# A causal hybrid decoder layer on one Trainium2 core: first queries and keys of three branches moved into the gate stage's block products

## The chip, the cores and the metric

One core of one Trainium2 chip runs the whole layer as one program. The metric is the device time of an execution in microseconds. Engines: PE (TensorE), DVE (VectorE), ACT (ScalarE), POOL (GpSimd) and SP (SyncE, which issues most DMAs).

## The reference

Input x is 1024 tokens by 1024 channels, fp32. One layer is x <- LN(a x + mixer(x)), then x <- LN(a x + ConvGLU(x)). The mixer runs four attention branches of 8 heads of 64 on one projection x W_in:

- A: window of 128 keys, 2 key heads, learned sinks, distance penalty;
- B: mixture of three dilations, own keys per head;
- C: each query takes its 256 best keys by an indexer score; one key and value head for all 8 query heads (`k` and `v` stand side by side in W_in, so one tile of 128 columns holds both);
- D: forgetting attention, with a cumulative log gate as bias.

Each branch's 512 outputs go through a projection to 1024 channels and are multiplied by sigmoid(x W_gate + b_gate) of that branch; the four products are summed and go through W_out.

```
proj   = einsum('bsnk,nkd->bsnd', branches, w_branch)
gates  = sigmoid(x @ w_gate + b_gate).reshape(b, L, 4, 1024)
merged = sum(gates * proj, axis=2);  y = merged @ w_out
```

## The kernel before, in words

fp32 precision is reached with pairs: every operand of a matmul is split into a high part (ACT copies it to fp32r, `*_hi`) and a low part (DVE or POOL subtracts, `*_lo`), and each product is three matmuls (high*high, high*low, low*high) of 128x128 by 512 columns. A projection of 128 output channels for all 1024 tokens (`project_parts`, L911) is 8 blocks of the inner size x 3 x 2 halves = 48 matmuls.

The order of the work is a written list, `STEPS` (`steps()`): x, indexer, `scores` (the indexer's scores), `gates`, then for each branch in the order B, D, A, C: first queries and keys (`q`, `k`; for C `kv_c` and `q`), values (`v` or `v_c`), four `attn` steps (one for a pair of heads), `osplit`, `merge`. Then `outproj`, `up`, `down`. Every engine's program walks the same list; engines meet only at semaphores, and each engine takes its own instructions in order.

**Gate stage** (`gates`, PE at L1225). The gate logits are made two tiles of 128 channels at a time (`GATE_TILES`, 22 tiles, 11 pairs) by block products: seven products of 12 matmuls each, with sums of weight blocks (POOL, `gate_weight_sums`) and of token blocks (made once), where two plain projections would take eight times 12. DVE combines the products (five operations a pair, L2694), ACT applies the sigmoid, SP stores the tile to DRAM. Between its combinations DVE runs parts of C's top-k search (`topk_parts`, `TOPK_GATES`: 14 parts a pair): the search has 191 parts, and 36 more (`topk_distances`, six per block of queries, six blocks of 384 to 1024 columns) turn the scores into distances. What the gate stage doesn't hold of them is spread over the merges (`TOPK_MERGE`) and the first projections (`TOPK_FIRST`).

**A branch's beginning.** PE projects the first queries and keys into two-bank PSUM tiles `pair[0]` and `pair[1]`; ACT scales and writes the high part into `heads` (`q_hi`, `k_hi`, L1675), DVE the low part (`q_lo` L2519, `k_lo` by `lo_part` L2648; each key row block twice, r = 0, 1). They read PSUM. Then `v`: of the value projection's eight parts of 6 matmuls PE runs five, the scores of unit 0, two more parts, the scores of unit 1, and the rest. A unit is 128 queries of one head; DVE adds its bias and takes the row minimum (`biased`, L2504), ACT exponentiates (`exps`, L1777), DVE takes the reciprocal (`inverse`, L2514), POOL normalises (L2230), PE transposes (L1000), ACT and DVE split the transposes (`pt_hi`, L2578), PE multiplies with the values (L1021). Projections of the next pair of heads are the filler between these (L927, plans `BESIDE`). For C there is no `v` projection: the key/value tile is staged and transposed (`v_c`, L963), four filler parts of 3 matmuls follow (`FIRST_C`), then the first units.

**Merge.** PE multiplies the branch's output with `w_branch` (L1247, L1254, L1271): eight tiles of 24 matmuls in four PSUM places; DVE multiplies each tile with its gate (L2957) and, for D and A, adds it to the sum `mid` (L2962). Gate tiles come back from DRAM into `prob[:, 0:2]` and `o_t[:, 0:4]` (`gate_home`, loads at L1476). Weights of the ring come through `w_raw` (SP, L1410), are split by ACT (L1652) and POOL (L2175), each tile as soon as the one two places earlier is used up: ACT splits one more as soon as the merge's last tile is done.

PSUM tile `pair[0]` holds the scores of one or two units: a unit marked by `scores_beside` waits until all but the last unit before it were read by `biased`, any other until all were.

## Time and profile before

| | |
|---|---|
| time, median of 3 runs | 2093.43 us (2091.26 to 2094.61) |
| profiled execution, its own time | 2093.97 us |
| its span | 2092.2 us |
| busy: PE, DVE, ACT, POOL | 2060.4, 1536.4, 968.5, 937.3 us |
| granted PE clock, mean | 0.999 |

How to read it: PE, DVE, ACT and POOL busy times are sums over instructions; a share of the span says little about a stage. The chain that ended last says which engine each moment of the span hangs on. Matmuls overlap: a row's mean duration is longer than the step from one matmul to the next, so PE's pace is read from a stretch and its count. A wait is put down to the engine whose signal came last.

### The profile page before, as it was taken

Reading aid. Unit: us, or ns where it says so; the run is one execution under the profiler, and the core shown is the slowest. Engines: PE = TensorE matmul, PEld = TensorE weight load, DVE = VectorE, ACT = ScalarE, POOL = GpSimd, SP = SyncE. Lnnn points to the kernel's source line nnn. Section 1 sums busy time; section 2 is a strip of 40 time slices with the busy share of each in tenths; the row PEclk is TensorE's granted clock in tenths of the full one; section 3 lists DMA queues with packets and bytes.
Section 4 is the critical chain, followed back from the end, with each engine's and each line's share of the span. In section 5 each row is a group of like instructions: output and inputs, shape, how many; then the busy total and the mean of one; then the engine's idle time right before and its main releaser. Section 6 shows DMA issues by size and latency. Waiting matters only on the chain.

```text
span 2092.2 us, 28999 instructions
## 1 busy us (share of the span) xinstructions
PE 2060.4 (98%) x10382; PEld 1727.0 (83%) x10382; DVE 1536.4 (73%) x2549; ACT 968.5 (46%) x1740; POOL 937.3 (45%) x796
## 2 busy tenths in 40 slices
PE   9999999999999999999999999999999999999998
PEld 7788888888888888888888888888788888888887
DVE  8678887777686666797785666668877777775668
ACT  5543334566615556615635666523433333344540
POOL 4287752333322223324523333524756565645651
PEclk9999999999999999999999999999999999999999
DMA  4233323110042111230031000441566665558862
GB/s 132 72 111 110 101 91 62 31 31 21 26 152 64 50 32 51 75 100 28 22 121 31 21 21 11 141 161 61 180 181 203 191 192 161 171 189 310 270 215 92
DMA packets 197373, 224.26 MB, mean 107 GB/s; under 512 B 25704, under 2 KB 149608, under 8 KB 197232
## 3 DMA queue, kind: packets, MB, share of 16 engines
q1 hardware_dynamic: 194320, 212.43, 32.7%
q10 hardware_dynamic: 2912, 10.00, 1.3%
q8 instruction: 83, 1.36, 0.3%
q14 instruction: 58, 0.48, 0.1%
HBM read 164.17 MB, written 58.23 MB: 106 GB/s over the span
## 4 chain that ended last, share of the span: by engine, by line
PE 87%; DVE 7%; issue 2%; ACT 2%; POOL 1%; DMA 0%; DVEq 0%; ACTq 0%; POOLq 0%
PE pair L1359 13%; PE pair L927 13%; PE pair L911 7%; PE pair L1225 7%; PE obank L1359 5%; PE pair L1388 5%; PE obank L1021 4%; PE chunk L1000 4%; PE pair L1318 3%; PE chunk L1388 3%; PE obank L1225 3%; PE pair L972 3%; PE pair L973 3%; PE pair L1271 2%; PE obank L1388 2%
## 5 line engine op out<-in xcount | busy, mean ns | idle before, releaser
L2175 POOL TENSOR_TENSOR w_lo<-w_raw,w_hi 128x1024 fp32r<-128x1024 f32 x64 | 159.5, 2492 | 311.1 <-ACT w_hi L1652 311.0
L1675 ACT ACTIVATE pt_hi<-chunk 128x512 fp32r<-128x512 f32 (+1 forms) x272 | 150.8, 555 | 179.2 <-PE chunk L1000 177.8
L2578 DVE TENSOR_TENSOR pt_lo<-chunk,pt_hi 128x512 fp32r<-128x512 f32 (+1 forms) x272 | 173.2, 638 | 80.1 <-ACT pt_hi L1675 75.7
L2230 POOL TENSOR_SCALAR prob<-prob,att 128x256 f32<-128x256 f32 (+4 forms) x172 | 118.1, 696 | 198.5 <-DVE att L2514 198.2
L927 PE MATMUL pair<-act_hi,w_hi 128*128 128x512 f32 x432 | 186.4, 432 | 2.5 <-DVE heads L2519 2.3
L927 PE MATMUL pair<-act_hi,w_lo 128*128 128x512 f32 x432 | 170.0, 393 | 0.0
L927 PE MATMUL pair<-act_lo,w_hi 128*128 128x512 f32 x432 | 169.4, 392 | 0.0
L2399 DVE TENSOR_SCALAR_CACHE_REDUCE o_top<-score,stat 128x384 uint8<-128x384 f32 (+1 forms) x186 | 167.0, 941 | 0.5
L1021 PE MATMUL obank<-pt_hi,heads 128*128 128x256 f32 (+1 forms) x568 | 148.4, 285 | 0.6 <-DVE pt_lo L2578 0.6
L1777 ACT ACTIVATE prob<-prob,att 128x257 f32<-128x257 f32 (+6 forms) x172 | 120.5, 702 | 39.3 <-DVE att L2504 38.0
L1021 PE MATMUL obank<-pt_lo,heads 128*128 128x256 f32 (+1 forms) x568 | 138.6, 281 | 0.0
L972 PE MATMUL pair<-heads 128*128 128x512 f32 (+3 forms) x352 | 119.9, 347 | 5.7 <-DVE att L2504 4.8
L911 PE MATMUL pair<-act_hi,w_hi 128*128 128x512 f32 x288 | 116.8, 405 | 5.0 <-DVE act_lo L2648 2.7
L1652 ACT ACTIVATE w_hi<-w_raw 128x1024 fp32r<-128x1024 f32 x64 | 67.4, 1053 | 111.8 <-PE obank L1271 38.3
L1000 PE MATMUL chunk<-ident,prob 128*128 128x128 f32 x660 | 111.9, 274 | 2.7 <-DVE pt_lo L2578 2.1
L1021 PEld LDWEIGHTS obank<-pt_lo,heads 128*128 128x128 f32 x568 | 108.2, 190 | 6.8
L1021 PEld LDWEIGHTS obank<-pt_hi,heads 128*128 128x128 f32 x568 | 107.4, 189 | 7.7 <-DVE pt_lo L2578 1.1
L973 PE MATMUL pair<-heads 128*128 128x512 f32 (+3 forms) x352 | 113.1, 334 | 0.0
L911 PE MATMUL pair<-act_lo,w_hi 128*128 128x512 f32 x288 | 112.6, 391 | 0.0
L911 PE MATMUL pair<-act_hi,w_lo 128*128 128x512 f32 x288 | 111.0, 392 | 0.0
L2230 POOL TENSOR_SCALAR mid<-mid,att 128x384 f32<-128x384 f32 (+4 forms) x56 | 37.8, 683 | 162.4 <-DVE att L2514 162.4
L927 PEld LDWEIGHTS pair<-act_hi,w_lo 128*128 128x128 f32 x432 | 81.1, 188 | 18.6
(489 smaller groups left out, 5932.5 us busy)
## 6 DMA issues: line engine op xcount, KB each, us to landing
down_sums<-dn_sums SPq DMA_DIRECT2D x40, 512.0 KB, 6.4
w_raw<-in_w_in SPq DMA_DIRECT2D x37, 512.0 KB, 3.8
gates<-o_t SPq DMA_DIRECT2D x22, 512.0 KB, 2.9
up_raw<-in_w_up SPq DMA_DIRECT2D x22, 512.0 KB, 4.8
gate_raw<-in_w_ffn_gate SPq DMA_DIRECT2D x22, 512.0 KB, 6.0
hidden<-gelu_s SPq DMA_DIRECT2D x22, 512.0 KB, 3.3
dn_raw<-down_sums SPq DMA_DIRECT2D x44, 256.0 KB, 4.1
h_in<-down_sums SPq DMA_DIRECT2D x44, 256.0 KB, 4.8
```

The source lines that it names most:

```text
L911: last = nc.tensor.matmul(dst[0:cols, s:s + HALF], w[:, k, :], a[:, k, s:s + HALF], start=(i == 0), stop=(i == len(order) - 1))
L927: last = nc.tensor.matmul(pair[1][:, s:s + HALF], w[:, k, :], a[:, k, s:s + HALF], start=(k == 0 and n == 0), stop=(k == NKT - 1 and n == 2))
L972: nc.tensor.matmul(dst[:, s:s + m], q, k_hi[:, s:s + m], start=True, stop=False)
L973: last = nc.tensor.matmul(dst[:, s:s + m], q, k_lo[:, s:s + m], start=False, stop=not masked)
L1000: last = nc.tensor.transpose(t[:, at:at + P], prob_slot(br, 2 * j + w)[:, s:s + P], ident[:])
L1021: last = nc.tensor.matmul(obank[bank_of(br)[j] % 2][:, q0:q0 + width], v, part[:, slot, at:at + width], start=(c == 0 and b == 0 and w == ...
L1225: last = nc.tensor.matmul(place, w[:, tokens_of(k)], gate_tokens(p, part, k), start=(p in (1, 6, 5) and k == 0 and m == 0), stop=(k == 3 a ...
L1359: last = nc.tensor.matmul(dst, w[:, cols], moving, start=(p in (1, 6, 5) and k == 0 and m == 0), stop=(k == 3 and m == 2), skip_group_chec ...
L1388: last = nc.tensor.matmul(banks[t], l[:, t * P:(t + 1) * P], r, start=(p in (6, 1, 5, 3) and k == 0 and m == 0), stop=(k == KFF - 1 and m ...
L2175: nc.gpsimd.tensor_tensor(split_into(1, g), w_raw[:, g % 2, 0:kt * cols], split_into(0, g).bitcast(F32), ALU.subtract).then_inc(lo_ready, 1)
L2399: nc.vector.tensor_scalar(junk[:, b % 2, 0:(i + 1) * P], s, limit if isinstance(limit, float) else limit[:, b:b + 1], None, ALU.is_ge, ALU ...
L2578: nc.vector.tensor_tensor(pt_lo[:, n % PT_SLOTS, 0:m], t[:, 0:m], pt_hi[:, n % PT_SLOTS, 0:m].bitcast(F32), ALU.subtract).then_inc(chunk_f ...
```

## The change

- `GATE_TILES` gets six more tiles, `HEAD_TILES`: queries and keys (for C the key/value tile) of D, A and C, the first 128 columns of each. They are made in the gate stage by block products, in three more pairs (14 in all), copied without the sigmoid, and stored to a DRAM tensor `first_heads`.
- The steps `q`, `k`, `kv_c` of D, A and C are replaced by a step `heads`. SP loads the two tiles into `o_t[:, 0]` and `o_t[:, 1]` once the fourth tile of the running merge is gated. ACT waits for the end of the merge on PE and writes the high parts: columns 0 to 511 of the first head and its keys, then 512 to 1023, then the second head and its keys. DVE writes the low parts in the same order, with the merge's last gated tile after the first half; then in `v`: other half, unit 0, second head, unit 1, reciprocal, staging copy. For C: first half, last gated tile, `v_c`, units 0 and 1, other half, second head, reciprocal, units 2 and 3. A semaphore `first_placed` counts these three pieces; PE waits for them before units 0, 4 and 8.
- PE starts the value projection right after the merge, and the scores of unit 0 stand after three of its parts for D and A instead of five.
- The whole top-k search is in the gate stage. Of the distance parts 24 (four blocks) stand in B's merge, 12 in D's, none in A's. POOL's sinks and bias for A wait for single gated tiles of D. ACT's spill of the last tile of B's merge moves behind the first heads' halves.

```diff
-TOPK_MERGE = {B: (2, 3), D: (1, 2), A: (0, 1), C: (0, 0)}
-TOPK_FIRST = {("k", D): 7, ("q", D): 6, ("k", A): 5, ("q", A): 5}
+EARLY_ROWS = 4
+LATE_DISTANCES = 5
+ROWS_BESIDE = 6
...
+HEAD_TILES = [(what, br) for br in BRANCH_ORDER[1:] for what in ("q", "k")]
+GATE_TILES = [(br, dt) for br in BRANCH_ORDER for dt in STORED_GATES[br] if (br, dt) not in FILLER_GATES] + HEAD_TILES
...
+        out += [("q", br, 0), ("k", br, 0)] if br == B else [("heads", br)]
...
                 if (br, pr) == (C, 0):
                     fill(FIRST_C)
+                    pe.wait_ge(first_placed, placed_first(br, 1))
                     scores(br, pr, 0)
                     scores(br, pr, 1)
...
+                        if p == 0 and br != B and u in (4, 8):
+                            pe.wait_ge(first_placed, placed_first(br, u // 4 + 1))
...
-                if merge_tiles.n and kind in ("q", "k", "kv_c", "outproj"):
+                if merge_tiles.n and kind in ("v", "v_c", "outproj"):
                     pe.wait_ge(merge_free, merge_tiles.n - 1)
...
                 elif kind == "v":
                     tile = project_parts(1, act_hi, act_lo)
-                    for _part in range(NKT // 2 + 1):
+                    for _part in range(NKT // 2 + 1 if step[1] == B else NKT // 2 - 1):
                         next(tile)
+                    if step[1] != B:
+                        pe.wait_ge(first_placed, placed_first(step[1], 1))
                     scores(step[1], step[2], 0)
...
+            def load_heads(br):
+                at = BRANCH_ORDER.index(br) - 1
+                if at == 0:
+                    sp.wait_ge(merge_free, 4)
+                else:
+                    sp.wait_ge(sum_done, sums_of(BRANCH_ORDER[at]) + 4)
+                for what in ("q", "k"):
+                    tile = GATE_TILES.index((what, br))
+                    sp.wait_ge(gate_stored[tile % 2], 16 * (tile // 2 + 1))
+                    sp.dma_start(first_head(what), tile_kept((what, br))).then_inc(heads_loaded, 16)
...
+            def first_heads(br):
+                at = BRANCH_ORDER.index(br)
+                act.wait_ge(merge_full, NKT * at)
+                act.wait_ge(heads_loaded, 32 * at)
+                first_half(br, 0)
+            def first_half(br, s):
+                q_hi(br, 0, 0, first_head("q")[0:HD, half_cols(s)], half_cols(s))
+                k_hi(0, first_head("k")[0:HD, half_cols(s)], cols=half_cols(s))
+            def other_heads(br):
+                first_half(br, 1)
+                if br == D:
+                    act.wait_ge(merge_free, merge_at(B) + NKT)
+                    spill(NKT - 1)
+                q_hi(br, 0, 1, first_head("q")[HD:P, :])
+                if br != C:
+                    k_hi(1, first_head("k")[HD:P, :])
...
-                    if step[:2] == ("k", A):
+                    if step == ("heads", A):
+                        pool.wait_ge(sum_done, sums_of(D) + NKT - 2)
+                        make_bias(0)
+                        pool.wait_ge(sum_done, sums_of(D) + NKT - 1)
+                        set_sinks(0, 0)
                         pool.wait_ge(sum_done, sums_of(D) + NKT)
...
+            def first_half(br, s):
+                q_lo(br, 0, 0, first_head("q")[0:HD, half_cols(s)], half_cols(s))
+                k_lo(0, first_head("k")[0:HD, half_cols(s)], cols=half_cols(s)).then_inc(first_placed, 1)
+            def first_heads(br):
+                before = BRANCH_ORDER[BRANCH_ORDER.index(br) - 1]
+                first_half(br, 0)
+                gated(before, NKT - 1)
+                dve.wait_ge(merge_free, merge_at(before) + NKT)
+                if before != B:
+                    dve.wait_ge(sum_done, sums_of(before) + NKT)
+            def other_head(br):
+                last = q_lo(br, 0, 1, first_head("q")[HD:P, :])
+                if br != C:
+                    last = k_lo(1, first_head("k")[HD:P, :])
+                last.then_inc(first_placed, 1)
...
                 elif kind == "v":
+                    if step[1] != B:
+                        first_half(step[1], 1)
+                    biased(step[1], step[2], 0)
+                    if step[1] != B:
+                        other_head(step[1])
+                    biased(step[1], step[2], 1)
+                    inverse(step[1], 0)
...
+                        if br == B and dt < ROWS_BESIDE:
+                            topk_parts(EARLY_ROWS * DISTANCE_PARTS // ROWS_BESIDE)
+                        elif br == D:
+                            topk_parts(((NSC - EARLY_ROWS) * DISTANCE_PARTS - LATE_DISTANCES) // (NKT - 1))
```

## Rows read from the trace of the kernel before

**Rows 1.** The page's first and fourth parts: busy time; the chain that ended last, by engine.

```profile
PE 2060.4 (98%) x10382; PEld 1727.0 (83%) x10382; DVE 1536.4 (73%) x2549; ACT 968.5 (46%) x1740; POOL 937.3 (45%) x796
...
PE 87%; DVE 7%; issue 2%; ACT 2%; POOL 1%; DMA 0%; DVEq 0%; ACTq 0%; POOLq 0%
```

**Rows 2.** What PE waited for (us in total, times, longest us); the largest.

```profile
PE pair L972 <- DVE att L2504: 4.8, 12, 0.8
```

**Rows 3.** Stretches: us, busy us of each engine (instructions), granted clock, DMA share, GB/s.

```profile
105.00:314.44 209.44, 209.44 (x925) 173.42 (x925) 178.74 (x426) 77.82 (x121) 151.09 (x118) 1.00 0.34 104
...
571.78:615.58 43.80, 43.80 (x195) 36.17 (x195) 36.22 (x71) 9.32 (x10) 9.65 (x4) 1.00 0.55 181
615.58:637.35 21.77, 21.77 (x97) 18.03 (x97) 18.82 (x42) 4.06 (x4) 4.81 (x2) 1.00 0.37 120
637.35:650.93 13.58, 13.16 (x64) 10.26 (x63) 7.07 (x11) 7.53 (x10) 3.21 (x3) 1.00 0.15 39
876.87:920.84 43.97, 43.90 (x193) 35.93 (x193) 40.88 (x46) 9.15 (x10) 10.48 (x4) 1.00 0.57 192
...
1098.26:1120.03 21.77, 21.77 (x99) 17.98 (x98) 8.41 (x6) 4.17 (x4) 4.80 (x2) 1.00 0.18 49
```

**Rows 4.** The page's sixth part: DMA issues, KB each, us from issue to landing.

```profile
w_raw<-in_w_in SPq DMA_DIRECT2D x37, 512.0 KB, 3.8
```

**Rows 5.** DVE's timeline in D's merge, distance parts: start us, us, instruction.

```profile
928.17 1.01 DVE L2441 TENSOR_SCALAR_CACHE_REDUCE o_top<-score,stat 128x768 uint8<-128x768 f32 x1
...
931.86 1.02 DVE L2452 SCALAR_TENSOR_TENSOR prob<-aux,stat,prob 128x768 f32<-128x768 f32 x1
```

**Rows 6.** ACT's timeline at B's merge end and in D.

```profile
615.67 1.06 ACT L1652 ACTIVATE w_hi<-w_raw 128x1024 fp32r<-128x1024 f32 x1 [9.82 <-PE obank L1271]
...
667.49 1.19 ACT L1675 ACTIVATE heads<-pair 64x512 fp32r<-64x512 f32 x2
```

**Rows 7.** DVE's timeline in D, A and C.

```profile
668.78 1.38 DVE L2648 SCALAR_TENSOR_TENSOR heads<-pair,heads 64x512 fp32r<-64x512 f32 x2 [0.80 <-ACT heads L1675]
...
933.97 4.93 DVE L2648 SCALAR_TENSOR_TENSOR heads<-pair,heads 64x1024 fp32r<-64x1024 f32 x4 [1.08 <-ACT heads L1675]
...
952.63 0.48 DVE L2504 CUSTOM_DVE_ANT_0 prob<-pair,o_t,sink_neg 128x256 f32<-128x256 f32 x1 [0.77 <-PE pair L973]
...
954.01 1.23 DVE L2889 COPY prob<-pair 128x1024 f32<-128x1024 f32 x1
...
1098.40 1.22 DVE L2957 TENSOR_TENSOR prob<-obank,prob 128x1024 f32<-128x1024 f32 x1 [2.65 <-PE obank L1271]
1099.66 3.32 DVE L2962 SCALAR_TENSOR_TENSOR mid<-mid,prob 128x1024 f32<-128x1024 f32 x1
...
1126.18 0.54 DVE L2504 CUSTOM_DVE_ANT_0 aux<-pair,score 128x384 f32<-128x384 f32 x1
...
1126.64 0.68 DVE L2504 CUSTOM_DVE_ANT_0 prob<-pair,score 128x512 f32<-128x512 f32 x1
```

**Rows 8.** POOL's timeline at the ends of B's and A's merge.

```profile
616.81 2.41 POOL L2175 TENSOR_TENSOR w_lo<-w_raw,w_hi 128x1024 fp32r<-128x1024 f32 x1 [8.48 <-ACT w_hi L1652]
...
1099.50 2.40 POOL L2175 TENSOR_TENSOR w_lo<-w_raw,w_hi 128x1024 fp32r<-128x1024 f32 x1 [8.48 <-ACT w_hi L1652]
```

**Rows 9.** DVE's sums, L2962: ns least/median/most, first and last start.

```profile
L2962 DVE SCALAR_TENSOR_TENSOR mid<-mid,prob x8: 1224/1226/3382, 887.4 to 1099.7; 128x1024 f32<-128x1024 f32 x8
```

**Rows 10.** PE's timeline: A's first transposes and filler, C's first and fifth score.

```profile
954.95 0.55 PE L1000 MATMUL chunk<-ident,prob 128*128 128x128 f32 x3 [0.51 <-POOL prob L2230]
955.29 0.49 PE L927 MATMUL pair<-act_hi,w_hi 128*128 128x512 f32 x1
...
1123.73 0.33 PE L972 MATMUL pair<-heads 128*128 128x128 f32 x1
...
1127.39 0.50 PE L972 MATMUL pair<-heads 128*128 128x512 f32 x1 [0.76 <-DVE att L2504]
```

**Rows 11.** The last stretch of the span, columns as in rows 3.

```profile
2080.00:2092.20 12.20, 4.72 (x21) 3.57 (x19) 8.44 (x16) 0.41 (x2) 0.00 (x0) 0.91 0.27 105
```

More of the change, by code:

```diff
@@ L794, in gate_bias_of, with tile_weights, tile_kept, first_head @@
             return gate_bias[:, br * NKT + dt:br * NKT + dt + 1]
+        def tile_weights(tile):
+            if tile not in HEAD_TILES:
+                return w_tile(w_gate[0], tile[0] * D_MODEL + tile[1] * P, P)
+            what, br = tile
+            return w_tile(w_in[0], Q_COL[br] if what == "q" else CK if br == C else K_COL[br], P)
+        def tile_kept(tile):
+            return heads_dram[HEAD_TILES.index(tile)] if tile in HEAD_TILES else gates_dram[tile]
+        def first_head(what):
+            return o_t[:, 0 if what == "q" else 1, :]
+        def placed_first(br, part):
+            return 3 * (BRANCH_ORDER.index(br) - 1) + part
         gate_out = [o_t[:, 2, :], o_t[:, 3, :]]
@@ L1518, in _ @@
                                  allow_slow_non_contiguous=True).then_inc(late_params, 16)
+                if step[0] == "heads":
+                    load_heads(step[1])
                 for n, source in enumerate(ring_sources(step)):
@@ L1726, in gate_operands, with gate_made_of @@
                     nc.scalar.activation(gate_operand(q, 0), gate_source(n, p), ACT.Copy).then_inc(gate_op_hi, 1)
+            def gate_made_of(n, k, dst, src):
+                tile = GATE_TILES[2 * n + k]
+                if tile in HEAD_TILES:
+                    return nc.scalar.activation(dst, src, ACT.Copy)
+                return nc.scalar.activation(dst, src, ACT.Sigmoid, bias=gate_bias_of(*tile))
             def take_first(n):
@@ L2832, in _ @@
                         counted(9)
-                    topk_parts(TOPK_FIRST.get(step[:2], 0))
-                    if step == ("q", D, 0):
-                        dve.wait_ge(pair_free[0], tiles[0].n)
-                        signal().then_inc(bias_used, 2)
                     k = step[1] in (B, D)
@@ L2969, in merged_lo @@
                     def merged_lo(k):
                         lo_part(act_lo[:, k, :], mid[:, k, :], act_hi[:, k, :]).then_inc(split_done, 1)
-                    topk_parts(start_parts)
-                    for dt in range(NKT):
+                    if br == D:
+                        topk_parts(LATE_DISTANCES)
+                    elif br == A:
+                        own(nc.vector.tensor_copy(dist_a[:], dist[:, SEQ - 2 * P:SEQ]))
+                    for dt in range(NKT if br == FINAL else NKT - 1):
```

188 lines of the change are left out of this document (79 added, 109 removed).

## The prediction

> **What bounds the kernel now.** I read the page first: PE is busy 98% of the span and carries 87% of the chain that ended last, DVE 7% [rows 1]. So PE work taken away is time, if nothing new makes PE wait. PE's waits are small: its largest, for DVE's biased scores, is 4.8 us in all [rows 2]. Then the table by stretch: the gate stage runs 924 matmuls of 128x512 in 209.44 us, and the 96 of D's first queries and keys take 21.77 us with PE never idle [rows 3]; both give 0.2268 us a matmul. (The rows' mean of some 0.39 us is latency, not the price.) In the same table DVE is busy 36.22 of 43.80 us in B's merge, but only 8.41 of the 21.77 us after A's merge: there queries and keys of C shelter a nearly idle DVE. Last I read the timelines around the three merge ends, since the change removes just this shelter. Below, T is the end of a merge on PE: 615.58 us (before D), 920.84 (A), 1098.26 (C) [rows 3].
>
> **Projections.** Removed: six projections (queries and keys of D and A, queries and the key/value tile of C) of 48 matmuls = 288 x 0.2268 = 65.3 us. Added: six tiles = three pairs of seven products of 12 matmuls = 252, 57.2 us. Sum: minus 8.16 us. Each new pair brings DVE five combinations and 14 search parts, ACT and POOL seven operands, POOL four sums; that is the load of the eleven pairs of now, which all run at PE's pace (19.04 us a pair, 209.44 / 11), so I charge nothing. If that cover failed, the excess of one engine over 19.04 us would be paid three times; no row shows an excess. The same three pairs swallow the 39 search parts that now stand in the merges, and the last pair has three parts fewer, which only moves work under B's first projection, again full.
>
> **Queues.** SP stores six more tiles of 512 KB in the gate stage and loads them again, each pair of loads behind the fourth gated tile and ahead of the value weights. With 5.44 us of PE a merge tile (24 matmuls) that is some 18 us before T. A load of 512 KB lands in 3.8 us [rows 4], and ACT splits the value weights two tiles, 11 us, before T, so all three are there; cost 0. Cover gone, ACT's placing would be late by what is missing, and then the first score unit. D's bias loads queue behind them, with 10 us to spare. ACT's fourth spill moves behind half of its placing; the D step waits there for the last gated tile. POOL's sinks and bias for A now follow its weight split; needed only some 8 us later: 0.
>
> **Merges.** B's merge gives DVE 24 distance parts in place of 26 search parts; four parts of the widest row, 768 columns, run from 928.17 to 932.88, 4.7 us [rows 5]. With the gating of 1.2 us that is 5.9 us against 5.44 us of PE a tile, but narrower rows go first, and my tally for six tiles (22 us of parts, 8 us of gating, 2 to 4 us of blocks as below) ends with the seventh tile gated about 1 us before T. The value projection waits for that tile. I take 0, with 2 us as the other end. D's merge has 12 parts instead of 17, A's none instead of 8: 0.
>
> **The merge ends.** Here is the cost. Once PE is done (T), ACT first splits a weight tile (615.67, 1.06 us) and only then can place; one half of the first queries and keys is three operations of 0.6 us, so ACT ends at T+2.8 [rows 6]. DVE's low parts of the same half are three of 0.61 to 0.69 us (two took 1.38 us) [rows 7]. They now read both operands from SBUF, where the removed ones read PSUM. And POOL subtracts the same weight tile from T+1.23 to T+3.64 [rows 8]. A DVE sum of two SBUF tensors takes 1.23 us alone, and 3.32 us when it starts beside such a subtraction, ending 1.1 us after it [rows 7 to 9]. So DVE's first low part ends at T+4.2 and the half at T+5.5; without the block it would be T+4.15. The nearest rows have 128 partitions, not 64; I take the block, since every sum that met a subtraction shows it, and keep 1.3 us as the other end.
>
> What the row shows, the Trainium skill's page "SBUF — State Buffer", section "SBUF: two separate sides", states as a rule: a VectorE operation with two SBUF inputs and a GpSimd operation that reads SBUF take one port pair for the whole instruction, and the loser fully blocks. By it the sum is the one with the block, whatever the partitions; without it each transition would be 1.3 us cheaper.
>
> **D.** PE needs the first half at T+4.08 (18 matmuls) and gets it at T+5.5: 1.4 us lost. The value projection then ends at T+13.0. DVE meanwhile: gating to 6.7, other half to 8.7, unit 0 to 9.1, then the other head, three operations of 1.2 us, waiting for ACT (10.3 after its own spill) to 12.8, unit 1 to 13.2. ACT's exponential, reciprocal and POOL's normalising follow as in A, where the transposes begin 1.8 us after unit 1's sum (953.1 to 954.95) [rows 7, 10]: here at T+15.1, where scores 2 and 3 end at 14.0. Another 1.1 us. Now PE loses 0.4 us in this stretch (busy 13.16 of 13.58 us) [rows 3]. Net 1.4 + 1.1 - 0.4, rounded up for semaphores: +2.2 us.
>
> **A.** The same, and DVE's sum of the last tile of D (1.2 us) also stands ahead. First unit: 1.4 us lost, value projection ends at T+12.8. DVE: gating and sum to 8.0, half to 10.0, unit 0 to 10.4, other head to 14.0, unit 1 to 14.6, reciprocal 15.5, staging copy (1.23 us) to 16.7 [rows 7]. PE stands before score 3 until 14.6, before the transposes until 16.3 and before the filler until 16.7, that is 3.9 us after the projection's end, where it now is 1.4 us (two scores 0.5, wait 0.51, transposes 0.34) [rows 10]. Net 1.4 + 2.5 = +3.9 us.
>
> **C.** No value projection shelters anything: transposes and 12 filler matmuls end at T+3.8, in the trace 3.7 us from 1120.03 to 1123.73 [rows 3, 10]. The first half comes at T+5.5 (+1.8). Then on DVE: gating and sum to 7.9, values to 8.7, units 0 and 1 to 9.0 and 9.4. Score 2 waits for unit 0, so it starts at T+9.1. DVE goes on with the other half to 11.4, the other head's queries to 12.6, reciprocal, units 2 and 3 (0.54 and 0.68 us) to 14.0 [rows 7]. Score 4 spans both banks and waits for unit 3, so it starts at T+14.1, behind it in PE's order all of the attention. From first to fifth score that is 8.6 us, now 3.66 us (1123.73 to 1127.39) [rows 10]. Net 1.8 + 4.9 = +6.7 us.
>
> **Sum.** -8.2 + 2.2 + 3.9 + 6.7 = +4.6 us, 12.8 us of new waits. The profiled execution took 2093.97 us, so 2098.6; it stands 0.54 us above the median of 2093.43, so I predict 2098.1. Ends: without the block the waits are 8.9 us (+0.7); with 2 us in B's merge and 1 us in POOL's bias work beside A's placing they are 15.8 us (+7.6).
>
> **Rivals.** (1) The waits are covered and the work leaves: if DVE and ACT finish each half inside the 4.08 us and C's units keep their old pace, only some 1 to 2 us come back, time 2086.5. PE's full stretches speak for it [rows 3], DVE's unit costs against it [rows 7]: C's DVE list from T to score 4 adds up to 11 us by itself, with 7.4 us of PE work beside it. (2) No block: placing is not hit, or POOL comes later. The sum then is +0.7, time 2094.1; what the sums show of two SBUF operands speaks against it [rows 7 to 9]. (3) The charge is halved in A and C because parts of the lists overlap better than my serial tally; 2.2 + 2.0 + 3.4 - 8.2 = -0.6, time 2092.8. (4) The clock falls. PE's granted clock is 1.00 in every stretch above [rows 3], but 0.91 in the last 12.2 us, where PE is busy 4.72 us and then idle to the end [rows 11]: it does fall to 1.2 GHz after idling. In C's stretch from T+3.8 to T+14.1 PE works some 2 us of 10. If it falls there, that work and the next few us run at half speed: 2 + 2 us more, 2102.1. It decides only if C's waits are as long as I say. The Trainium skill, "TensorE: Matmul & The Clock Gate", Part 1, states that the array drops to half clock when it has been idle and comes back only after sustained work; by it this rival would be likely here, and no row of this trace shows such a fall ahead of work. (5) The change does not do what it says: value projections start at T in all cases, and only the first units move; the moved projections are real matmuls either way, so this is no case of its own.
>
> **Chances.** Forecast 0.42 (own range 2095.5 to 2101); rival 1 0.13, rival 2 0.20, rival 3 0.12, rival 4 0.13. A measurement of this kernel can tell some 0.2%, 4.2 us: faster is below 2089.2, slower above 2097.6. Rival 1, and a small tail of 3, are faster: 0.15. Rivals 2 and 3 are within, and three tenths of the forecast, which straddles the bound: 0.43. The rest of it and rival 4 are slower: 0.42. Range 2090 to 2103: it takes in rivals 2, 3 and 4 and leaves out rival 1 and the far end of 4, under 0.2.
>
> **What would show it.** PE matmuls of the gate stage 1176 in 266.6 us, no longer any of the six projections. In the waits of PE, about 13 us more for DVE's placed heads and biased scores: over 1 us before the first unit of D, A and C, 1 to 2.5 us before the transposes of D and A, two waits of some 3 us each in C before the third and the fifth score. DVE's first 64x512 low part after each merge longer than 2 us. It is wrong if C's fifth score starts less than 10 us after the merge's end, or if PE waits longer in the gate stage or at the value projection's start; the granted clock of C's first 20 us decides rival 4.

## The result and the profile after

The changed kernel takes 2113.47 us (median of 5 runs, 2112.2 to 2117.59), the kernel before 2093.43 (5 runs): ratio 1.0099, 95% interval 1.0085 to 1.0114, so 1.0% slower. I had predicted 2098.1, in 2090 to 2103: the sign was right, the size was not. The profiled execution took 2112.2 us, its span is 2110.1: it is the quickest of the five, and 1.3 us under their median. First the page after, its first and fourth parts, beside [rows 1]:

```profile
PE 2058.9 (98%) x10346; PEld 1724.6 (82%) x10346; DVE 1551.4 (74%) x2572; ACT 983.3 (47%) x1776; POOL 965.5 (46%) x823
...
PE 82%; DVE 10%; issue 3%; ACT 2%; DMA 2%; POOL 2%; DVEq 0%; SPq 0%; ACTq 0%; POOLq 0%
```

36 matmuls fewer, as announced, and only 1.5 us less of busy PE (at 0.2268 us each it should be 8): some now run slowly. The chain gained DVE and, new, DMA. The largest waits of PE (us in total, times, longest us), beside [rows 2]:

```profile
PE pair L986 <- DVE heads L2705: 10.0, 4, 5.8
PE pair L986 <- DVE att L2559: 9.8, 13, 3.0
PE pair L925 <- DVE mid L2858: 3.9, 1, 3.9
PE chunk L1014 <- POOL prob L2282: 1.4, 2, 1.3
```

L986 is a score's first matmul, "heads" DVE's low parts of queries and keys, "att" a biased score, L925 the value projection and "mid" a gated tile. To find in which stretch the time went, I cut both traces where PE begins a stage: B's projection, then the first instruction behind the merges of B, D and A, less the wait ahead of it. Before (columns as in [rows 3]):

```profile
0.00:314.27 314.27, 308.57 (x1410) 255.88 (x1411) 254.01 (x515) 135.98 (x215) 190.52 (x152) 1.00 0.34 103
314.27:615.41 301.14, 298.54 (x1649) 253.62 (x1648) 218.44 (x416) 158.39 (x292) 91.05 (x80) 1.00 0.20 53
615.41:920.68 305.27, 303.23 (x1713) 254.73 (x1712) 216.82 (x408) 158.27 (x292) 90.66 (x83) 1.00 0.20 64
920.68:1098.10 177.42, 172.75 (x961) 149.48 (x960) 138.42 (x277) 89.34 (x214) 69.91 (x147) 0.99 0.18 54
1098.10:2092.20 994.10, 977.31 (x4653) 813.29 (x4651) 708.70 (x935) 426.56 (x727) 495.11 (x334) 1.00 0.46 147
```

and after:

```profile
0.00:371.00 371.00, 365.37 (x1662) 302.42 (x1663) 303.44 (x634) 156.33 (x248) 232.25 (x185) 1.00 0.35 105
371.00:672.38 301.38, 298.75 (x1649) 253.46 (x1647) 218.91 (x383) 158.41 (x292) 91.85 (x80) 1.00 0.19 53
672.38:970.87 298.49, 285.89 (x1617) 240.06 (x1617) 210.06 (x366) 156.54 (x293) 86.68 (x81) 0.98 0.22 69
970.87:1129.65 158.78, 149.94 (x865) 129.98 (x864) 111.51 (x255) 87.61 (x215) 67.01 (x145) 1.00 0.19 61
1129.65:2110.10 980.45, 958.98 (x4557) 798.72 (x4555) 707.46 (x936) 424.38 (x728) 487.73 (x332) 0.99 0.46 148
```

What stands ahead of B's projection grew by 56.73 us, with 252 matmuls more. D, A and C each lost 96 matmuls, 21.77 us, and should have come to 283.50, 155.65 and 972.33 us. What each has over that is its loss:

| stage | predicted | measured |
|---|---|---|
| ahead of B's projection, less six projections | -8.16 | -8.6 |
| B | 0 | +0.2 |
| D | +2.2 | +15.0 |
| A | +3.9 | +3.1 |
| C | +6.7 | +8.1 |
| sum | +4.6 | +17.9 |

The sum is the difference of the two profiled executions; the medians differ by 20.0 us. The gate stage itself, from its first matmul (104.83 us before, 104.44 after), grew from 209.44 to 266.56 us, so by 57.12 us; the other 0.4 us of the first line comes from ahead of it.

Nearly all that I missed is in D. Its timelines in the changed kernel, SP, ACT, POOL and DVE in this order (T, the merge's end, is 672.4):

```profile
658.69 0.42 SPq L1427 DMA_DIRECT2D w_raw<-in_w_in  x1
675.02 0.80 SPq L1539 DMA_DIRECT2D aux<-c_forget  x2
675.86 11.73 SPq L1427 DMA_DIRECT2D w_raw<-in_w_in  x3
...
683.71 1.06 ACT L1677 ACTIVATE w_hi<-w_raw 128x1024 fp32r<-128x1024 f32 x1 [17.88 <-DMA w_raw<-in_w_in]
684.68 3.61 ACT L1700 ACTIVATE heads<-o_t 64x512 fp32r<-64x512 f32 x6
...
665.91 2.40 POOL L2227 TENSOR_TENSOR w_lo<-w_raw,w_hi 128x1024 fp32r<-128x1024 f32 x1 [9.90 <-ACT w_hi L1677]
684.85 2.34 POOL L2227 TENSOR_TENSOR w_lo<-w_raw,w_hi 128x1024 fp32r<-128x1024 f32 x1 [16.54 <-ACT w_hi L1677]
...
666.02 2.71 DVE L2499 TENSOR_SCALAR prob<-score,stat 128x768 f32<-128x768 f32 x1
674.88 0.06 DVE L2411 MEMSET stat<- 128x1 f32 x1
674.96 1.22 DVE L2858 TENSOR_TENSOR mid<-pair,prob 128x1024 f32<-128x1024 f32 x1
685.32 2.42 DVE L2574 SCALAR_TENSOR_TENSOR heads<-o_t,heads 64x512 fp32r<-64x512 f32 x1 [9.14 <-ACT heads L1700]
```

Read it from the end. D's first scores start at 689.19, T+16.8, because DVE's low parts begin at 685.32, because ACT's placing begins at 684.68. ACT had nothing to do for 17.88 us: it stood at the split ahead of the placing, whose weight landed only at 683.7. SP issued that load at 675.86, behind D's two bias loads, for which it had waited since 659: they need DVE's signal (the memset at 674.88), which follows DVE's last distance part. Four loads of 512 KB (two bias loads, this weight and, at 676.34, the next) then shared the DMA engines, whose share was full (1.04 in the first line below), and the load took 7.8 us and not the 3.8 of [rows 4].

The kernel before has the same stall on SP, from 608.7 to 625.3, and there it costs nothing (its SP, then its ACT):

```profile
608.36 0.37 SPq L1410 DMA_DIRECT2D w_raw<-in_w_in  x1
625.34 0.81 SPq L1511 DMA_DIRECT2D aux<-c_forget  x2
...
641.56 1.06 ACT L1652 ACTIVATE w_hi<-w_raw 128x1024 fp32r<-128x1024 f32 x1
```

The weight behind the bias loads was split there only at 641.56, T+26, because the weights of D's two projections came first. The change took these two out of the ring, so the same weight is now due at T.

Besides, the seventh gated tile was done at 676.18, so the value projection began 3.85 us after T. And the clock fell (same columns as above):

```profile
676.23:683.00 6.77, 6.77 (x17) 5.35 (x18) 0.00 (x0) 0.00 (x0) 0.00 (x0) 0.55 1.04 299
683.00:689.19 6.19, 0.42 (x2) 0.00 (x0) 3.81 (x4) 4.50 (x7) 2.34 (x1) 0.72 0.16 38
689.19:693.00 3.81, 3.81 (x12) 3.13 (x13) 3.69 (x7) 2.18 (x3) 0.00 (x0) 0.57 0.64 227
...
1140.00:1144.00 4.00, 2.28 (x6) 1.28 (x4) 3.91 (x9) 0.61 (x3) 0.83 (x2) 0.50 0.00 0
1144.00:1148.00 4.00, 3.79 (x12) 3.24 (x13) 1.53 (x6) 2.21 (x7) 1.23 (x2) 0.50 0.00 0
```

0.50 is 1.2 GHz, half of 2.4. PE had waited 3.85 us before the first of these stretches and 5.78 in the second; in C it had waited 2.03 us up to 1135.4 and 2.97 us up to 1139.1, ahead of the last two.

### The profile page after: what moved, and what is told of

The parts are those of the page before. It is cut to its first block, busy times and chain, and to the rows that moved or that the text cites. A ratio compares the mean times of both kernels' runs of the same rounds, so it can differ in the third digit from the quotient of the medians.

```text
span 2110.1 us, 29071 instructions
## 1 busy us (share of the span) xinstructions
PE 2058.9 (98%) x10346; PEld 1724.6 (82%) x10346; DVE 1551.4 (74%) x2572; ACT 983.3 (47%) x1776; POOL 965.5 (46%) x823
## 3 DMA queue, kind: packets, MB, share of 16 engines
q8 instruction: 83, 1.36, 0.3%
## 4 chain that ended last, share of the span: by engine, by line
PE 82%; DVE 10%; issue 3%; ACT 2%; DMA 2%; POOL 2%; DVEq 0%; SPq 0%; ACTq 0%; POOLq 0%
PE pair L1376 13%; PE pair L941 13%; PE pair L1242 9%; PE obank L1376 5%; PE obank L1035 4%; PE chunk L1014 4%; PE pair L1405 4%; PE pair L925 4%; PE obank L1242 4%; PE pair L1335 3%; PE pair L986 3%; PE pair L987 3%; PE chunk L1405 2%; PE obank L1405 2%; PE pair L1288 2%
## 5 line engine op out<-in xcount | busy, mean ns | idle before, releaser
L2227 POOL TENSOR_TENSOR w_lo<-w_raw,w_hi 128x1024 fp32r<-128x1024 f32 x58 | 148.0, 2551 | 270.4 <-ACT w_hi L1677 270.3
L941 PE MATMUL pair<-act_hi,w_hi 128*128 128x512 f32 x432 | 187.1, 433 | 2.5 <-DVE heads L2574 2.3
L941 PE MATMUL pair<-act_hi,w_lo 128*128 128x512 f32 x432 | 170.5, 395 | 0.0
L941 PE MATMUL pair<-act_lo,w_hi 128*128 128x512 f32 x432 | 170.1, 394 | 0.0
L986 PE MATMUL pair<-heads 128*128 128x512 f32 (+3 forms) x352 | 121.1, 350 | 19.8 <-DVE heads L2705 10.0
L1677 ACT ACTIVATE w_hi<-w_raw 128x1024 fp32r<-128x1024 f32 x58 | 61.1, 1053 | 124.4 <-DMA w_raw<-in_w_in 52.2
L1376 PE MATMUL pair<-t,op_late 128*128 128x512 f32 x396 | 95.4, 390 | 1.0 <-POOL op_late L2237 0.7
L986 PEld LDWEIGHTS pair<-heads 128*128 128x128 f32 x352 | 67.4, 191 | 35.4 <-DVE att L2559 12.8
L1376 PE MATMUL pair<-t,op_early 128*128 128x512 f32 x396 | 95.1, 389 | 0.2 <-DVE up_s L2751 0.2
```

Source lines behind the costliest of these rows:

```text
L941: last = nc.tensor.matmul(pair[1][:, s:s + HALF], w[:, k, :], a[:, k, s:s + HALF], start=(k == 0 and n == 0), stop=(k == NKT - 1 and n == 2))
L986: nc.tensor.matmul(dst[:, s:s + m], q, k_hi[:, s:s + m], start=True, stop=False)
L1376: last = nc.tensor.matmul(dst, w[:, cols], moving, start=(p in (1, 6, 5) and k == 0 and m == 0), stop=(k == 3 and m == 2), skip_group_chec ...
```

## The experiments

Four theories. **1**: SP's order holds back a weight, and ACT's split of it the placing. **2**: DVE's serial list and the port it shares with POOL set the waits in A and C. **3**: DVE is overloaded beside B's merge. **4**: the clock falls because of the waits, and costs on its own. Rivals stand in the expectations. "Over" is a stage's length less 283.50, 155.65 or 972.33 us, in the one profiled execution of each kernel. Such a figure scatters: before D's value projection, behind the same code of PE and DVE, PE waits 3.85 us in the changed kernel and 2.75, 3.16, 2.32, 2.71 and 3.19 in e1, e2, e4, e5 and e7. Each group of kernels was timed beside the kernel before, so the ratios compare them best.

| kernel | median us | ratio to before (95%) | over: D | A | C |
|---|---|---|---|---|---|
| changed kernel | 2113.47 | 1.0099 (1.0085 to 1.0114) | 15.0 | 3.1 | 8.1 |
| e1_bias_order | 2104.79 | 1.0051 (1.0034 to 1.0068) | 5.1 | 6.3 | 7.0 |
| e2_place_first | 2110.82 | 1.0079 (1.0062 to 1.0096) | 11.2 | 1.5 | 5.7 |
| e3_three_rows | 2113.26 | 1.0094 (1.0079 to 1.0109) | 8.7 | 12.2 | 7.8 |
| e4_five_parts | 2114.27 | 1.0101 (1.0086 to 1.0116) | 12.3 | 6.3 | 8.0 |
| e5_order_and_place | 2104.05 | 1.0055 (1.0040 to 1.0070) | 5.1 | 4.6 | 7.6 |
| e6_parts_ahead | 2102.33 | 1.0052 (1.0037 to 1.0067) | 3.1 | 3.1 | 8.8 |
| e7_spread_c | 2113.36 | 1.0097 (1.0082 to 1.0112) | 14.9 | 7.4 | 5.9 |
| e8_together | 2099.78 | 1.0033 (1.0020 to 1.0045) | 4.2 | 4.7 | 4.9 |
| e9_dve_order | 2097.84 | 1.0021 (1.0012 to 1.0030) | 2.1 | 4.0 | 4.2 |
| e10_kept_busy | 2111.94 | 1.0089 (1.0075 to 1.0103) | 13.1 | 3.1 | 5.6 |
| e11_dve_order_again | 2098.29 | 1.0024 (1.0014 to 1.0033) | 5.2 | 3.9 | 4.1 |
| e12_busy_in_a | 2096.75 | 1.0021 (1.0012 to 1.0030) | 2.3 | 2.4 | 4.1 |

One timed execution of e1_bias_order took 11753.93 us; it is not in the ratio. The kernels whose interval lies clear below that of the changed kernel (e1, e5, e6, e8, e9, e11, e12) are those that contain e1's edit. On top of it, only the whole of e9, e11 and e12 is clear of e1; no single further step is clear of the one before.

**e1_bias_order.** SP's order alone.

```
-                if step == ("v", D, 0):
-                    forget_bias(0)
-                    forget_bias(1)
...
                     load_weights(source)
+                    if n == 0 and step == ("attn", D, 0):
+                        forget_bias(0)
+                        forget_bias(1)
```

> Edit: in the changed kernel SP issues D's two bias loads behind the next weight load, not before it. Theory 1 (at the head of D, SP's wait for DVE's signal ahead of the bias loads holds back the next weight load, ACT's split of that weight stands before its placing, and so the first scores come at T+17): SP issues the weight load some 6 us before T instead of 3.7 us after it, ACT splits at about T, the wait before D's first scores falls from 5.78 us to under 1.5; the wait of 3.85 us before D's value projection stays. Time 5 to 9 us under the changed kernel, about 2106. Rival (DVE's own list and the port shared with POOL are what is late): the first scores still wait over 4 us, time within 1.5 us of the changed kernel.

D shrank by 9.9 us and the median by 8.7: theory 1. The first scores start at 680.83, T+8.6 and not T+16.8, with no wait of their own, though DVE's first low part is still hit by POOL. The wait before the value projection, ahead of which the edit changes nothing, is 2.75 us for 3.85; so 1.1 of the 9.9 us is scatter. ACT's timeline, then DVE's:

```profile
672.37 1.06 ACT L1677 ACTIVATE w_hi<-w_raw 128x1024 fp32r<-128x1024 f32 x1 [6.34 <-PE obank L1288]
673.34 3.61 ACT L1700 ACTIVATE heads<-o_t 64x512 fp32r<-64x512 f32 x6
...
675.00 1.42 DVE L2574 SCALAR_TENSOR_TENSOR heads<-o_t,heads 64x512 fp32r<-64x512 f32 x1
```

ACT's split is now released by PE's last merge tile and no longer by a DMA.

**e2_place_first.** ACT places before it splits, after all three merges.

```
                         merged_hi(NKT - 1)
-                    else:
-                        ahead()
...
                 first_half(br, 0)
+                ahead()
```

> Edit: in the changed kernel ACT places the first half of the heads before it splits the next weight, behind all three merges; the order of SP's loads stays. Theory 1 expects the same gain in D as from the other order of SP (the first scores' wait under 1.5 us, 5 to 9 us), although the weight still lands late. Theory 2 (POOL's split, released by ACT's, blocks DVE's first low parts in A and C) expects besides that DVE's first 64x512 low part takes under 1 us in A and C instead of 2.4 to 2.5, and that the waits of 1.76 us (A) and 2.03 us (C) before the first scores go. Together about 2102. Rival to theory 2: the low parts stay over 2 us or the wait only moves to the next scores, and A and C gain under 1 us together.

In D the wait of 5.78 us went, but only 3.8 us of the stage did: the weight was as late as before, and its split now stood ahead of ACT's next pieces, so PE waited 3.30 and 0.96 us at +20 and +22. ACT's timeline in D:

```profile
672.86 1.80 ACT L1700 ACTIVATE heads<-o_t 64x512 fp32r<-64x512 f32 x3 [7.27 <-PE obank L1288]
683.21 1.06 ACT L1677 ACTIVATE w_hi<-w_raw 128x1024 fp32r<-128x1024 f32 x1 [8.54 <-DMA w_raw<-in_w_in]
```

In A and C theory 2 held. DVE in C, where the changed kernel had 2.47 us for the same instruction, and PE's waits there:

```profile
1125.52 0.69 DVE L2573 SCALAR_TENSOR_TENSOR heads<-o_t,heads 64x512 fp32r<-64x512 f32 x1 [3.55 <-ACT heads L1700]
1126.76 1.39 DVE L2704 SCALAR_TENSOR_TENSOR heads<-o_t,heads 64x512 fp32r<-64x512 f32 x2 [0.56 <-ACT heads L1700]
...
PE pair L986 <- DVE att L2558: 5.7, 2, 3.8
```

No block, no wait before the first scores; the third waits longer instead (3.76 for 2.97 us). So the block is real: 2.4 to 2.5 us against 0.69 for one instruction. What it is worth is less sure. A and C came down by 1.6 and 2.4 us in the profiled execution, but the edit also takes ACT's split of 1.06 us out of the way, and that execution (2104.75 us) is the quickest of the four; the median moved by 2.7 us, inside the scatter, and in e5 the same edit on top of e1 gains nothing that can be told (ratios 1.0055 and 1.0051).

**e3_three_rows.** One row of distance parts moves from B's merge to D's.

```
-EARLY_ROWS = 4
-LATE_DISTANCES = 5
+EARLY_ROWS = 3
+LATE_DISTANCES = 4
```

> Edit: in the changed kernel B's merge carries three rows of distance parts (3 a tile) and not four (4 a tile); D's merge takes the other row (4 parts first and 2 a tile). Theory 3 (DVE has too much beside B's merge): the wait of 3.85 us before D's value projection falls under 0.5 us and the granted clock stays at 1.00 there; DVE's signal comes some 3 us earlier and with it the weight load, so D's first scores come about 3 us earlier. Time 3 to 5 us under the changed kernel, about 2109.5. A may lose up to 1.5 us of it, its merge having 7 parts more. Rival (the wait before the value projection is hidden by the later one): D's first scores come at the same time as before, time within 1 us.

Missed, and telling. D's wait before the value projection went and D fell by 6.3 us; but the row did to D's merge what it had done to B's. PE's waits in D, then at the start of A:

```profile
PE pair L986 <- DVE heads L2705: 5.7, 1, 5.7
...
PE pair L925 <- DVE prob L2858: 6.2, 1, 6.2
```

A lost 9.1 us: the 6.16 us, and slices of the clock at 0.50 and 0.57 behind. Six parts more (one more behind each of seven tiles, one fewer ahead of them; I had written seven) made DVE 6.16 us late where I had allowed 1.5: D's merge was full too. In D the first scores came at T+10.0, 6.9 us sooner where I had expected 3, so the rival (the wait is hidden by the later one) falls. Theory 3 holds for both merges.

**e4_five_parts.** The one part of the change that was named: scores behind three or five parts.

```
-                    for _part in range(NKT // 2 + 1 if step[1] == B else NKT // 2 - 1):
+                    for _part in range(NKT // 2 + 1):
```

> Edit: in the changed kernel the first scores of D and A stand behind five parts of the value projection again, not behind three. The theories 1 to 3 all say that the scores are held by the placing, not by their place: D's wait before the first scores falls from 5.78 us by the 12 matmuls put before it (2.7 us at full clock), A's 1.76 goes, and the same time comes back as waits at the scores and transposes behind. Time within 1.5 us of the changed kernel. Rival (putting them sooner is itself what costs): 3 us or more are gained.

As expected: the wait before D's first scores fell to 3.88 us; A's 1.76 is gone and the wait before its fourth score grew from 1.67 to 3.71; and the time is the same. (In the profiled execution D is 2.7 us shorter, 1.5 of it ahead of the value projection, and A 3.2 longer, with slices at 0.50 and 0.63.) Where the first units stand is worth nothing that can be measured while the placing sets them.

**e5_order_and_place.** e1 and e2 together.

> Edit: both earlier ones together, SP's bias loads behind the weight load and ACT's first half before its split. Theory 1 says that the two are one cause in D, seen from SP and from ACT, so D gains no more than the better of them alone (10 us with SP's order, D's stage 288.6 us), while A and C keep what ACT's order gave them (1.7 and 2.3 us). Time about 2101 to 2102.5. Rival (two separate causes in D): D's stage under 286 us, time under 2099.

D is 288.6 us as with e1 alone: one cause, seen from two engines. The time missed (2104.05): against e1, A is 1.7 us shorter and C 0.6 longer. C's fifth score waits 2.81 us where it waited 1.93, and the clock had slices at 0.67 and 0.57 in A and at 0.50 in C.

**e6_parts_ahead.** e1, and B's distance parts from ahead of the merge.

```
-ROWS_BESIDE = 6
+ROWS_BESIDE = 5
...
+                    if br == B:
+                        topk_parts(4)
...
-                            topk_parts(EARLY_ROWS * DISTANCE_PARTS // ROWS_BESIDE)
+                            topk_parts(4)
```

> Edit: on top of SP's order (e1), the 24 distance parts beside B's merge begin ahead of its first tile (4 parts there, 4 behind each of five tiles), in DVE's idle time, so that the last four stand behind the fifth tile and not behind the sixth. Theory 3 (DVE late with the seventh gated tile): the wait before D's value projection, 2.75 us with e1, goes, the granted clock stays at 1.00 from the merge's end on, DVE's signal and the bias loads come some 4 us sooner. 3 to 5 us under e1, about 2100.5. Rival (the late start was cover for the placing, so the wait moves to the first scores): D's stage within 1 us of e1's 288.6 us.

Missed. D fell 2.0 us under e1 in the profiled execution, the wait from 2.75 to 1.32 us, and the clock stayed at 1.00 in D. But the kernel's time did not move: the ratios are 1.0052 and 1.0051, and the medians differ only as those of the kernel before do (2092.64 and 2093.7). And the later kernels with the same edit have the wait at 2.49 (e8), 1.36 (e9) and 2.45 us (e11), as three (e6, e9) or four (e8, e11) of DVE's parts happen to meet POOL's splits. DVE was busy 37.97 of the 39.25 us from 635 to the seventh tile: it has too much to do there wherever the parts stand.

**e7_spread_c.** Filler between C's scores.

```
                 if pr == 0:
+                    if br == C:
+                        fill(5)
                     scores(br, pr, 2)
...
-BESIDE_C = (((0, 0), (0, 2), (1, 1), (1, 1), (2, 2), (3, 0), (3, 1), (6, 0), (6, 2), (8, 1),
+BESIDE_C = (((0, 0), (0, 0), (0, 0), (3, 0), (8, 1),
```

> Edit: in the changed kernel five of C's filler parts (3 matmuls each) stand between its second and third scores and two more ahead of its first group, taken from the groups behind; D, A and ACT's order stay. Theory 4 (in C, PE has nothing else to do while DVE works through its list, and the clock falls because of the waits): the waits of 2.97 and 1.93 us fall under 0.5 us together, the clock of the first 20 us of C stays at or above 0.9 instead of three slices at 0.50, and C's stage is 4 to 6 us shorter than the changed kernel's 980.4 us; time about 2108.5. Rival (the waits come back at the groups that lost their filler): under 1.5 us gained. Rival (the clock falls all the same, by the first wait of 2.03 us alone): 3 to 4 us gained and still slices at 0.50.

Missed. The two waits fell to 0.58 us and the slow slices from 0.53, 0.50, 0.50 and 0.76 to 0.71 and 0.87, but C gained only 2.2 us: as filler moved forward, later groups waited (0.66 us at +22.8, and small ones). The median did not move (2113.36); in D the first scores waited 6.70 us, and A was 4.2 us longer in the profiled execution, with slices at 0.51 and 0.64 that the changed kernel's had not.

**e8_together.** e1, e2, e6 and e7.

> Edit: the four together (SP's order, ACT's first half before its split, distance parts from ahead of B's merge, C's filler spread). If the causes add up: D's stage near 285 us, A's 157 to 159, C's 972 to 975, time 2086 to 2092, at or under the kernel before (2093.7). If some of them only moved waits about, it stays over 2095.

Missed: 2099.78 us is over the 2095 above which, I had written, some of the four only moved waits about. D is 287.7 us for 285, A 160.3 for 157 to 159 and C 977.2 for 972 to 975. The median is 5.0 us under e1's; in the profiled executions that is C (2.1) and A (1.6), while D is 0.9 shorter than with e1 and 1.1 longer than with e6. Still 0.33% slower than before.

**e9_dve_order** and **e11_dve_order_again.** On top of e8, another order of DVE's list. e9 in D and A:

```
                     biased(step[1], step[2], 0)
-                    if step[1] != B:
-                        other_head(step[1])
+                    q_lo(step[1], 0, 1, first_head("q")[HD:P, :])
                     biased(step[1], step[2], 1)
+                    k_lo(1, first_head("k")[HD:P, :]).then_inc(first_placed, 1)
                     inverse(step[1], 0)
```

and in C, all four biased scores ahead of the second half. e11 moves the second biased score and the reciprocal (inverse) further forward.

> Edit: on top of the four together (e8), DVE takes up the finished scores before it places what is needed later: in D and A the second biased score stands ahead of the other head's keys, in C all four stand ahead of the second half and the other head. Theory 2 as the runs have left it (what is left of the waits in A and C is DVE's serial list, and its order decides): A's waits of 2.06 and 1.26 us fall under 1.5 us together, C's of 1.95 us under 0.5, D's 0.86 goes; time 3 to 5 us under e8's 2099.8, about 2095.5. Rival (the work is the limit, not its order, so the waits come back at the scores and transposes behind): under 1 us gained.

> Edit: e9 with two places changed: in D and A the second score's bias comes directly behind the first's and the reciprocals stand ahead of the other head's keys, in C the second half is placed ahead of the fourth score's bias. In e9 the wait of 2.99 us before A's first transposes was for the reciprocals, which stood behind 2.45 us of placing. Expected if DVE's order decides: that wait falls to 0.5 to 1 us, the granted clock of A's start stays over 0.9, the waits in C fall from 1.9 to about 1.2; 2.5 to 4 us under e9's 2097.8, about 2094.5. If DVE's work as such is the limit: within 1 us of e9.

e9 gained 1.9 us in the median where I had expected 3 to 5, and the intervals of e8 and e9 overlap. Its waits in A became one of 2.99 us at the transposes, for the reciprocal behind 2.45 us of placing (DVE's timeline of e9, A):

```profile
970.95 2.45 DVE L2708 SCALAR_TENSOR_TENSOR heads<-o_t,heads 64x1024 fp32r<-64x1024 f32 x2
973.43 0.17 DVE L2570 RECIPROCAL att<-att 128x2 f32<-128x2 f32 x1
```

e11 moved it forward and the wait fell only to 2.35 us; its time is e9's, as its rival had it. (Its D is 3.2 us longer, with 1.1 us more wait before the value projection, ahead of the edit, and the clock at 0.57 behind it.) So neither order helped more than this; that DVE's and ACT's work as such is now the limit is the reading left, not a thing that a run with less of that work has shown.

**e10_kept_busy** and **e12_busy_in_a.** Matmuls that nobody reads, while PE waits: e10 in the changed kernel, e12 on top of e11.

```
+            def keep_busy(dst, n):
+                for _ in range(n):
+                    nc.tensor.matmul(dst, act_hi[:, 0, 0:P], act_hi[:, 0, 0:HALF], start=True, stop=True)
```

> Edit: in the changed kernel PE runs matmuls whose results nobody reads while it waits: 16 ahead of D's value projection, 20 ahead of D's first scores, 8, 10 and 6 ahead of C's first, third and fifth scores (a bank that is free, 0.227 us each). All waits on DVE stay. Theory 4 (the granted clock falls because of the waits): the clock is 1.00 all through both transitions; D's first scores still come at T+17, since DVE sets them, so the slow 18 matmuls ahead of them cost nothing and D gains 1.3 to 2 us; C gains 2 to 3.5 us; together 3.5 to 5 us under the changed kernel, about 2109. Rival (the clock falls for another reason): slices at 0.50 stay and the time is the same or longer.

> Edit: e11 with 6 matmuls that nobody reads in the wait before D's value projection and 8 ahead of A's first transposes. If the clock falls there because of the waits, what is left of it under 1.00 in A goes: 1 to 1.5 us under e11 where e11 still has a slice below 0.9 at A's start. If e11 has none, the 8 matmuls cost up to their 1.8 us less the wait they fill: e11 to e11 + 1 us.

The same stretches in e10:

```profile
676.00:680.00 4.00, 3.85 (x17) 2.86 (x16) 1.96 (x3) 0.00 (x0) 0.00 (x0) 1.00 0.45 124
...
1140.00:1144.00 4.00, 2.46 (x10) 1.39 (x8) 3.88 (x9) 0.62 (x3) 0.82 (x2) 1.00 0.00 0
1144.00:1148.00 4.00, 3.97 (x20) 3.20 (x21) 2.43 (x6) 2.24 (x7) 1.25 (x2) 1.00 0.00 0
```

The clock stays up, D is 1.9 and C 2.5 us shorter, as theory 4 said. Of D's 1.9 us the clock has only 0.8: the first scores came at T+15.7 and not T+16.8, because the weight landed in 6.6 us and not in 7.8, and only what is behind them ran faster. The medians show 1.5 us; in the profiled execution 2.0 are lost again before B's projection, which begins at 373.0 and not 371.0, and the intervals of the two kernels overlap. So that matmuls in the waits keep the clock up is shown; that it pays in the time of the kernel is not. In e12 the wait before A's transposes is 0.5 us and the clock of A's start 1.00 (PE's wait; then the slice that was at 0.57 in e11):

```profile
PE chunk L1019 <- POOL prob L2294: 0.5, 1, 0.5
...
976.00:980.00 4.00, 4.00 (x24) 3.43 (x23) 2.64 (x8) 2.46 (x8) 0.00 (x0) 1.00 0.00 0
```

Its median is 1.5 us under e11's, inside the scatter of the two. By the median it is the quickest variant, by the ratio it is level with e9, and still 0.21% slower than the kernel before.

## Why the prediction was wrong in size and right in sign

**Projections: right.** The gate stage ran 266.56 us where I had written 266.6; 57.12 us for 252 matmuls is 0.2267 each, PE's pace. Against six projections that is -8.2 us for -8.16.

**Queues: wrong; this is the step that failed.** I wrote that D's bias loads queue behind the heads' loads "with 10 us to spare". The spare time was that of the loads (they were issued at 657.84, 14.5 us before T where I had 18, and were in time). I did not follow what SP waits for ahead of them, DVE's signal, nor what stands behind them on SP, the next weight; and I had seen ACT's split ahead of the placing only as 1.06 us of work, not as a wait for a DMA. Nor did any rival have it. ACT's split was ready to start only at T+11.3 (683.71), where I had it at T, and the first scores came at T+16.8, where I had T+5.5. e1 prices it: 9.9 of D's 15.0 us, 8.7 us in the median (8.8 of the 9.9 without the scatter ahead of the edit).

**Merges: wrong by a smaller term.** I had the seventh tile gated 1 us before T, at worst 2 us late; it came 3.8 us late, and PE did wait at the value projection's start, which I had named as a sign of being wrong. Three of DVE's parts met POOL's splits and took about 2 us more each (2.71 for 0.62 us at 666.02), some 6 us where I had counted 2 to 4. How many meet is chance: in e1 it was two, and the tile came 2.7 us late. e6 shortens the wait, but no gain in the kernel's time can be told from it. For D's merge I had 0, and e3 shows that it had no room either. It also cost something at its start, 1.4 us in the changed kernel and in every variant but e3 (1.0); POOL's split of a weight, then PE's first matmul that needs it:

```profile
934.00 4.03 POOL L2227 TENSOR_TENSOR w_lo<-w_raw,w_hi 128x1024 fp32r<-128x1024 f32 x1 [11.45 <-ACT w_hi L1677]
...
938.13 0.70 PE L1288 MATMUL pair<-heads,w_hi 128*128 128x512 f32 x2 [1.41 <-issue]
```

The same split took 2.40 us in the kernel before, and PE did not wait there. Now DVE's distance parts run beside it; it takes 4.03 or 4.04 us wherever PE waits 1.4, and 3.58 in e3. (PE's program waits for this split; the profile names no releaser, so that it ended the wait is read from the times.)

**Merge ends, A and C: right, and closer in the sum than it should be.** DVE's first low part took 2.42, 2.40 and 2.47 us in D, A and C, so the block exists on 64 partitions; A's waits came at +6.0, +15.5 and +17.2 us where I had 5.5, 14.6 and 16.3, C's first, third and fifth score at +5.8, +9.5 and +14.6 for 5.5, 9.1 and 14.1. The losses are 3.1 and 8.1 us for 3.9 and 6.7. Two things that I had not in the sum are in them. The kernel before has a slice of 4 us inside A, from 1028 to 1032, with a granted clock of 0.57, which costs some 1.7 us (an estimate: 0.43 of 4 us); the changed kernel's profile has none in A; without that A's loss is 4.8 us, as its waits say (1.76 + 1.67 + 1.26). In C the clock has its part (below); the waits alone are about 5.6. That 3.1 + 8.1 comes so near 3.9 + 6.7 is in part luck. The rival without the block falls with the 2.4 to 2.5 us, and e2 shows that they are POOL's; the one in which all waits are covered falls with the table. D's +2.2 could not be seen: its first half came too late for another reason.

**The clock: the rival was right as a mechanism.** It fell in C as described and in D as well. I priced it at 4 us beyond the forecast, which would still have been in my range; e10 measures 2.5 us in C and 0.8 in D, in one execution. In D the slow projection cost nothing, as the scores behind it waited for DVE anyhow; only the matmuls after 689.19 count. I had also written that no row shows such a fall ahead of work; the trace of the kernel before has one, the slice of 0.57 at 1028, behind a wait of 1.7 us.

Left of D's 15.0 us after these: 2.1 us in e9. That this is nearly what I had forecast is chance: in e9 it is the wait before the value projection (1.36 us) and that at D's merge (1.40), less the 0.4 us that PE waited at D's start before. Not tried: the moved tiles of a single branch, and the three pairs alone in the kernel before, so the -8.2 us is read from the trace and not from a run of its own.

## What to carry to other kernels

Work that gives other engines time to catch up has a value of its own: six projections of 10.9 us stood where DVE and ACT had to catch up. Making them elsewhere saved 8.2 us, and even in the best variant the three stages together were 8.8 us (2.3 + 2.4 + 4.1) over what they should have been. When a load is moved or gets a new neighbour, write down for each instruction of that queue what it waits for and what stands behind it, and do so again when something is taken out of the queue: a stall that cost nothing can then stand ahead of a load that is due sooner; a wait for another engine's signal ahead of an unrelated weight load cost more here than everything saved. When an engine's list is tallied beside a merge, add a block for each of POOL's splits that falls into it.

## What the runs showed of the hardware that I had not expected

DVE's single-input TENSOR_SCALAR on SBUF is blocked by POOL's subtraction as well: 128x768 took 2.71 us beside it in the changed kernel (666.02) and 0.62 us without in e1 (665.94). The Trainium skill says why: "VectorE: DVE Perf Modes", section "Mode 2×_2P — use both read ports for one tensor", lets such an operation use both read ports, and by "SBUF — State Buffer", section "SBUF: two separate sides", an operation in that mode takes the pair it shares with GpSimd; the trace agrees, as the operation ended at 668.73, 0.42 us behind POOL's (665.91 and 2.40 us). The gating product, which has one input in PSUM, took 1.22 us beside a split in e9 (963.11), not longer.

The clock is not settled by the list of waits alone. With the same three waits at A's start (1.76, 1.67 and 1.26 us) it stayed at 1.00 in the changed kernel's profiled execution and fell to 0.88 and 0.69 for two slices of 4 us in e1's; and before D's value projection PE waited 2.49 us in e8 and 2.45 in e11, and the clock stayed at 1.00 in the first and fell to 0.57 in the second. Another such slice came some 90 us into A in most runs (0.77 and 0.80 in e1, whose A was 3.2 us longer by both falls together), as it does 107 us into A in the kernel before (0.57). PE waits 1.7 us there in the changed kernel too, and its clock did not fall. What decides it I leave open; it is part of why single executions of one kernel here differ by 2 to 7 us.
